# Twenty conditioning products moved out of the channel mixer into the stops around it, with the norms' root taken once per token

## What is computed

```
def rmsnorm(x, g):
    y = xf * lax.rsqrt(jnp.mean(xf * xf, axis=-1, keepdims=True) + RMS_EPS)
    return (y * g.astype(jnp.float32)).astype(x.dtype)
...
    for l in range(DEPTH):
        mod_x = (jax.nn.silu(c) @ w_ada[l] + b_ada[l])[:, None, :]
        mod_c = jax.nn.silu(c_ctx) @ w_ada[l] + b_ada[l]
        sh1, sc1, gt1, sh2, sc2, gt2 = jnp.split(mod_x, 6, axis=-1)
...
        hx = modulate(rmsnorm(x, g_pre_mix[l]), sh1, sc1)
        y_x, y_c = mixer_sublayer(hx, hc, ...)
        x = x + gt1 * rmsnorm(y_x, g_post_mix[l])
        hx = modulate(rmsnorm(x, g_pre_ffn[l]), sh2, sc2)
        x = x + gt2 * rmsnorm(channel_mixer(hx, l, ...), g_post_ffn[l])
```

## Time and profile before

| | us |
|---|---|
| median of 3 runs | 2317.41 (2314.95 to 2319.59) |
| the profiled execution | 2325.32 |
| its span, first to last instruction | 2323.5 |
| first mixer, up to the first stop | 0 to 578.6 |
| stop before the channel mixer | 578.6 to 605.0 |
| channel mixer | 605.0 to 1003.3 |
| stop behind it | 1003.3 to 1031.3 |
| second mixer | 1031.3 to 1356.3 |
| norms 5 and 6, router, gather | 1356.3 to 1391.2 |
| experts and end | 1391.2 to 2323.5 |

### The profile page before, as it was taken

The page is one execution under the profiler, slowest core; times in us unless marked ns, Lnnn a source line. Parts: engine busy times, 40 slices in busy tenths (PEclk is TensorE's granted clock), DMA queues, the critical chain, the costliest instruction groups (busy, mean ns, idle before and its releaser), DMA issues.

```text
span 2323.5 us, 55627 instructions
## 1 busy us (share of the span) xinstructions
PE 2260.5 (97%) x24638; PEld 1645.4 (71%) x24638; DVE 763.8 (33%) x1543; ACT 560.5 (24%) x1090; POOL 48.1 (2%) x63
## 2 busy tenths in 40 slices
PE   7999999999999999998999999999999999999999
PEld 4777877778678887868898986555555555555555
DVE  4465354543732223376647651000000000100002
ACT  4345343323322222234535430000000000000001
POOL 0000010000200000000011000000000000000000
PEclk8999999999999999999999989999999999999999
DMA  6323242224644344213333479999999999999992
GB/s 252 123 109 131 79 155 100 113 107 188 219 188 161 112 155 178 75 55 109 109 119 130 170 289 374 391 404 381 404 384 407 380 408 387 405 385 406 394 412 100
DMA packets 86185, 548.93 MB, mean 236 GB/s; under 512 B 10257, under 2 KB 13457, under 8 KB 25937
## 3 DMA queue, kind: packets, MB, share of 16 engines
q1 hardware_dynamic: 52880, 352.68, 39.4%
q10 hardware_dynamic: 28912, 178.14, 19.6%
q0 software_dynamic: 4176, 14.81, 2.0%
HBM read 529.08 MB, written 16.52 MB: 235 GB/s over the span
## 4 chain that ended last, share of the span: by engine, by line
PE 85%; DVE 9%; ACT 3%; issue 2%; DMA 1%; ACTq 0%; DVEq 0%; SPq 0%
PE S L1764 17%; PE O L1764 13%; PE pp L1439 9%; PE pp L1441 8%; PE pp L1440 8%; PE T L1764 8%; PE S L1439 2%; DVE wsp L971 2%; PE S L1440 2%; PE S L1441 2%; PE T L1440 2%; PE T L1441 2%; PE T L1439 2%; PE pp L1474 2%; PE T L1570 1%
## 5 line engine op out<-in xcount | busy, mean ns | idle before, releaser
L1764 PE MATMUL S<-slabs,M 128*32 128x256 f32 x7168 | 475.6, 380 | 1.4 <-issue 1.0
L971 DVE TENSOR_TENSOR wsp<-raw,wsp 128x1024 fp32r<-128x1024 f32 (+3 forms) x248 | 264.0, 1086 | 326.2 <-ACT wsp L631 325.0
L1764 PEld LDWEIGHTS S<-slabs,M 128*32 128x32 f32 x7168 | 231.3, 110 | 155.7 <-issue 13.4
L1439 PE MATMUL pp<-hx,wsp 128*128 128x512 f32 (+1 forms) x800 | 284.8, 356 | 20.2 <-DVE M L1182 4.7
L1764 PE MATMUL O<-slabs,M 128*32 128x256 f32 x5376 | 294.7, 379 | 0.0
L1394 DVE TENSOR_TENSOR M<-M,S 128x256 f32<-128x256 f32 x56 | 23.6, 421 | 807.0 <-ACT M L921 807.0
L1764 PE MATMUL T<-slabs,M 128*32 128x256 f32 x3584 | 279.2, 379 | 0.1
L1440 PE MATMUL pp<-hx,wsp 128*128 128x512 f32 (+1 forms) x800 | 277.4, 347 | 0.0
L1441 PE MATMUL pp<-hx,wsp 128*128 128x512 f32 (+1 forms) x800 | 277.3, 347 | 0.0
L1764 PEld LDWEIGHTS O<-slabs,M 128*32 128x32 f32 x5376 | 173.2, 110 | 114.9 <-issue 1.3
L631 ACT ACTIVATE wsp<-raw 128x1024 fp32r<-128x1024 f32 (+3 forms) x248 | 224.1, 935 | 30.7 <-PE pp L1441 19.6
(11 more groups left out here) (242 smaller groups left out, 2343.1 us busy)
## 6 DMA issues: line engine op xcount, KB each, us to landing
slabs<-in_w_moe SPq DMA_DIRECT2D x175, 1024.0 KB, 9.2
slabs<-in_w_moe ACTq DMA_DIRECT2D x161, 1024.0 KB, 9.2
raw<-in_w_main SPq DMA_DIRECT2D x84, 1024.0 KB, 5.0
M<-in_w_main SPq DMA_DIRECT2D x40, 1024.0 KB, 5.0
raw<-in_w_br SPq DMA_DIRECT2D x24, 512.0 KB, 3.6
xm<-in_w_main SPq DMA_DIRECT2D x8, 1024.0 KB, 5.2
raw<-in_w_dn SPq DMA_DIRECT2D x8, 768.0 KB, 4.2
moe_rows<-M POOLq DMA_DIRECT2D x14, 384.0 KB, 9.7
```

The costliest lines, as they stand in the source:

```text
L971: dve.tensor_tensor(wsp[:, slot, 1, 0:w], raw[:, rslot, half * w:half * w + w], wsp[:, slot, 0, 0:w], ALU.subtract).then_inc(lo_done, 1)
L1439: mm(dst, w_hi, x_hi, start=first, stop=False)
L1764: ins = mm(banks[g // 2][32 * c:32 * c + 32, 256 * (g % 2):256 * (g % 2) + 256], x(k, g), slab_e[i % RAW_E][:, 1024 * k + 256 * c:1024 * k ...
```

## The change

1. The 22 products and turns leave the channel mixer (`ffn`). Two of these slabs go beside the last tiles of the first mixer, whose plan now has 20 `ada` steps; the last turn stands before the output projection (`wout`).
2. Ten products and turns are written into each of the two stops (`stop`, `stop_product`, `stop_turn`), in place of most `keep_up` matmuls. Their slabs are loaded by `load_stop` into ten buffers of their own (`stop_buf`), some of which only come free when the stage before has ended.
3. In norms 1 to 6 the sum is taken with the squares as weights and one column of `mean` as data (`token_sums`), which leaves one number per token, 128 tokens down the partitions. Root and reciprocal then work on 4 columns (2 in norms 5 and 6). DVE multiplies the identity by each column (`dg`), and PE multiplies that by `mean` to spread the factors over all partitions into the PSUM bank `R` (`norm_cast`).
4. In norms 5 and 6 and in the router fewer constant matmuls stand in one block and more of them between the sums and the router's small matmuls.
5. POOL clears its scratch rows later (in the channel mixer), and three small DVE operations that prepare the second layer's factors stand behind norm 4.

```diff
+ADA_STOP = 10
+ADA_MIXER = [(0, s) for s in range(ADA_FIRST, ADA_SLABS)] + [(1, s) for s in range(ADA_SLABS - 2 * ADA_STOP)]
+STOP_PRODUCT = {0: 3, 1: 4, 2: 5, 4: 6, 5: 7}
+STOP_TURN = {0: 2, 1: 3, 2: 4, 3: 5, 5: 6, 6: 7}
...
             for g in range(2, N_SLABS):
+                if g == g_gu[0]:
+                    for n in range(4):
+                        load_stop(0, n, step_of[0, "wout", 0]["t"])
+                if g == g_gu[0] + 2:
+                    for n in range(4, ADA_STOP):
+                        load_stop(0, n, t_stop[0] if n < 8 else t_stop[0] + n - 7)
...
+                if g == g_mix[1] + 2:
+                    for n in range(6, ADA_STOP):
+                        load_stop(1, n, t_stop[1])
                 load(g)
...
+            def token_roots(n, N):
+                dve.wait_ge(sd_done, n + 1)
+                own.link(dve.reciprocal(root[:, 1, 0:N // P], root[:, 0, 0:N // P]))
+                for b in range(N // P):
+                    dve.tensor_scalar(dg[:, b, :], ident[:], root[:, 1, b:b + 1], float(D), ALU.mult, ALU.mult).then_inc(dg_done, 1)
+                dve.wait_ge(cast_done, n)
...
+            def token_sums(src, N, first, last):
+                for b in range(N // P):
+                    ins = mm(O[1][:, b:b + 1], src[:, P * b:P * b + P], mean[:, 0:1], ...)
...
+                token_sums(sq[:, 1, :], N, False, True).then_inc(sum_done, 4)
+                if n < 5:
+                    stop_product(n // 2, 0)
+                else:
+                    keep_up(5)
+                norm_cast(n, N)
...
+            def stop(b, n):
+                stop_product(b, 1)
+                stop_turn(b, 0)
+                stop_product(b, 2)
+                stop_turn(b, 1)
+                for k in range(KT):
+                    norm_sum(n, k, TOK)
+                    if k in STOP_PRODUCT:
+                        stop_product(b, STOP_PRODUCT[k])
+                    if k in STOP_TURN:
+                        stop_turn(b, STOP_TURN[k])
+                    if k in (3, 6):
+                        keep_up(2)
+                stop_product(b, 8)
+                norm_cast(n, TOK)
+                stop_product(b, 9)
+                stop_turn(b, 8)
+                keep_up(2)
+                stop_turn(b, 9)
...
             mixer(0, 1, 0)
-            keep_up(28)
-            for k in range(KT):
-                norm_sum(2, k, TOK)
-            keep_up(31)
+            stop(0, 2)
             ffn()
...
-            keep_up(16)
+            keep_up(6)
             for k in range(KT):
                 norm_sum(6, k, SEQ)
-            keep_up(31)
+                keep_up(5 if k == KT - 1 else 1)
+            norm_cast(6, SEQ)
+            keep_up(5)
...
-            ins.then_inc(rt_pe, 1)
+                if k == KT - 1:
+                    ins.then_inc(rt_pe, 1)
+                else:
+                    keep_up(1)
```

More of the change, by code:

```diff
@@ L128, in mixer_plan @@
             end = len(steps)
+    steps.extend(late)
     for n in range(0, KT, 2):
@@ L207, in build_program @@
         ada_c = view(M, 0, 2048)
-        ada_f = [view(M, 2048 * j, 2048) for j in range(2)]
+        ada_m = [view(M, 2048 * j, 2048) for j in range(2)]
+        stop_buf = [ada_m + [slabs[:, n, :] for n in (4, 5, 0, 1, 2, 3)] + ada_m,
+                    ada_m + [slabs[:, n, :] for n in (6, 7, 8, 9, 0, 1, 2, 3)]]
         def ada_rows(n):
@@ L331, in build_program @@
         g_gu, g_dn = [0, 0], [0, 0]
+        stop_main = [nmain, 0]
+        nmain += ADA_STOP
         for h in range(2):
             g_gu[h], u_gu[h] = len(order), units()
-            for _ in range(F_HALF[h]):
-                add("main", 1, 2048)
-                add("main", 1, 2048, True)
+            add("main", F_HALF[h], 2048)
             g_dn[h], u_dn[h] = len(order), units()
@@ L384, in build_program, with plan_stop @@
         t = ADA_FIRST
+        def plan_stop(b):
+            nonlocal t
+            t_stop[b], use_stop[b] = t, use[0]
+            t += ADA_STOP
+            for n in range(2):
+                use[n] += ADA_STOP // 2
         plan_mixer(0)
+        plan_stop(0)
         for h in range(2):
-            t_gu[h], use_gu[h] = t, use[0]
+            t_gu[h] = t
             for f in range(F_HALF[h]):
@@ L398, in build_program @@
                 use[b] += DN_STAGE // 2
+        plan_stop(1)
         plan_mixer(1)
@@ L416, in build_program @@
                 place(g, ada_c, 0, ada_use[ada_mix[n - 1]] if n > ADA_BESIDE_A else step_of[0, "vn", (1, 1)]["t"])
[L417 to L420, removed]
+        need = [max([last_use[n - 4] if n >= 4 else 0] + [ada_src[g][3] for g in ada_src if g < slab_of[n]]
+                    + ([step_of[0, "wout", 0]["t"]] if slab_of[n] >= g_gu[0] else [])) for n in range(N_UNITS)]
         end_of = [u_gu[0] + 2, N_UNITS]
@@ L710, in affine_step, with stop_row @@
                                    ).then_inc(affine, 1)
+            def stop_row(b, n):
+                act.wait_ge(tile_done, t_stop[b] + n + 1)
+                if n >= 2:
+                    act.wait_ge(cols_done, ADA_FIRST + ADA_STOP * b + n - 1)
+                act.activation(adr_f[:, n % 2, :], pp[n % 2][:, 0:256], ACT.Copy).then_inc(taken[n % 2], 1)
             def prenorm(n, l, which, N, hcount):
+                stop = {2: 0, 4: 1, 6: None}[n]
+                if stop is not None:
+                    stop_row(stop, 0)
+                    stop_row(stop, 1)
                 for k in range(KT):
@@ L1074, in prenorm @@
             def prenorm(n, l, which, N):
-                dve.wait_ge(sd_done, n + 1)
-                own.link(dve.reciprocal(rs[:, 0:N], sd[:, 0:N]))
+                token_roots(n, N)
                 for k in range(KT + 1):
@@ L1281, in _ @@
             postnorm(3, 0, 1, TOK, y)
-            dve.wait_ge(cols_done, ADA_FIRST + ADA_FFN)
-            own.link(mod_add(1, ADA_SLABS - ADA_FFN, O[0][:, 0:4 * ADA_FFN]))
-            for part in range(4):
+            dve.wait_ge(cols_done, ADA_FIRST + ADA_STOP)
+            own.link(mod_add(1, ADA_SLABS - 2 * ADA_STOP, O[0][:, 0:4 * ADA_STOP]))
+            for part in range(2):
                 own.link(am_part(1, part))
@@ L1457, in keep_up, with norm_cast @@
                     mm(bank[:, 0:P], mean[:], mean[:], start=True, stop=True)
+            def token_sums(src, N, first, last):
+                for b in range(N // P):
+                    ins = mm(O[1][:, b:b + 1], src[:, P * b:P * b + P], mean[:, 0:1], start=(first and b == 0), stop=(last and b == N // P - 1))
+                return ins
+            def norm_cast(n, N):
+                before = [0, 4, 8, 12, 16, 18][n - 1]
+                for b in range(N // P):
+                    pe.wait_ge(dg_done, before + b + 1)
+                    ins = mm(R[:, P * b:P * b + P], mean[:], dg[:, b, :], start=True, stop=True)
+                ins.then_inc(cast_done, 1)
@@ L1900, in _pack_dense @@
     dns, f = [], 0
+    for s in range(ADA_STOP):
+        ada(1, ADA_SLABS - 2 * ADA_STOP + s)
     for nF in F_HALF:
```

99 lines of the change are left out of this document (61 added, 38 removed).

## The result

The changed kernel takes 2323.65 us in the median of seven runs (2321.39 to 2327.73). The kernel before took 2317.3 us in seven runs on the same chip. The ratio is 1.0029 with a 95% interval of 1.0018 to 1.0039. I had forecast 2288.6 and a gain of 28.8 us. The change costs 6 us instead.

A forecast was written before the change was run, and what follows sets the result against it. PE was taken to bound most stages, the norms' ACT and DVE chain the old stops. -30.8 (channel mixer) + 6.0 (first mixer) + 4.2 (stops) - 8.2 (norms 5 and 6, router) = -28.8, from 2317.4 to 2288.6 us; range 2274 to 2303.

The forecast's parts named there:

- I take PE's sum, since each price is a row at full clock: Two stops: PE, not DVE, sets the pace, +2.1 us each, +4.2 for both.
- the last of the signs of being wrong: Stops: the prediction would be wrong if the clock there is below 1.00; it expected 1.00.
- my second rival: Stops: 12 us of each at clock 0.50 would cost 6, giving 2301 us; chance 0.12.
- The stops at full clock: Each stop +2.1 us: PE's pace costs +4.1, less 2.0 for the second root.
- the 2.3 among my signs: Stops: sums spaced at 2.3 us for the first blocks, as a sign in the profile after.
- The full drain on each side of a product: Stops: a pair of tiling-mode switches at 0.33 us, not 0.17; each stop 1.3 longer, result 2291.
- The root's gain: Stops: factors ready 2.1 us earlier at norm 1, 2.0 at norm 2; 4.1 a stop if nothing else changed.
- The channel mixer: Products and turns leave the tile boundaries: 28.8, 1.2 and 0.8 us, together -30.8.
- hidden work that turns into a wait: Channel mixer, behind a half's last tile: of 2.57 us only about 0.4 goes, since DVE's splitting chain ends late.
- The first mixer: Two more slabs in its last groups: +2.6, +1.3 and 2.1 us, sum +6.0; bounds 3.2 to 7.8.
- Norms 5 and 6 and the router: Roots 1.4 us, router pairs 4.5 earlier, gather 2.7, small steps about 1; sum -8.2.
- The loads: Stops: slabs land 5.0 us apart, no wait expected; rival of late loads, slower from 8.0 us spacing, chance 0.03.

The follow-up runs named there:

- norms_thin: Kernel before with slabs left in the channel mixer, norms merged with one-column sums, constants in the stops, router as changed; 2321.63 us, before 2317.73, ratio 1.0015.
- old_sums: Changed kernel with slabs still in the stops, but norms 1 to 4 as before (512-column sums, old roots); 2319.07 us, before 2321.18, ratio 0.9989.
- norms_wide: Same as norms_thin but with 128-column sums in the merged norms; 2307.92 us, before 2321.18, ratio 0.9943.
- wide_sums: Changed kernel with each sum of norms 1 to 6 multiplying by 128 equal columns, not one; 2300.27 us, before 2321.18, ratio 0.9913.
- twelve_bridged: twelve plus nine constants ahead of PE's wait behind each half of the channel mixer; 2295.21 us, before 2321.03, ratio 0.9883.
- more_constants: Changed kernel, thin sums kept, with two constants behind each of a stop's eight sums (16, not 4); 2313.31 us, before 2317.73, ratio 0.9976.
- twelve: wide_sums with twelve slabs in the second stop and none of the second layer's in the first mixer; 2293.73 us, before 2321.03, ratio 0.9882.
- wide_late_turn: wide_sums with the first mixer's last turn behind the first tile of the output projection; 2295.43 us, before 2317.73, ratio 0.9907.

## Why the prediction was wrong, point by point

**The step that failed** is "I take PE's sum, since each price is a row at full clock". The prices were nearly right and the clock was not. A clock below 1.00 in the stops was the last of the signs of being wrong that I had named. It is my second rival, "the clock falls in the stops", to which I gave 0.12, and it was mis-sized too. I had 12 us of each stop at 0.50, costing 6. The windows show 13.5 and 15.3 us lost. The slip in my 6 is plain: 12 us of work at half the clock take 24 and cost 12. PE sets the pace, so whatever it does at 0.50 takes twice as long. In the first stop that is some 13.5 us of work, from 597.4 to 624.7. The clock was back only behind the last thin sum of the stop, which ends at 621.27. So it was in the second stop (last sum's end 1034.7, full clock from 1037.2) and in both of norms_thin. With no thin sum ahead a fall was shorter: 6.6 us for the first of the second stop, 6 and 10 us behind the first gaps of old_sums. What brings the clock back was not tested. With 13.5 + 15.3 = 28.8 us lost in the stops in place of 12, that rival gives 2288.6 + 28.8 = 2317 and not 2301.

**Why I gave it 0.12.** I read 1.00 in the old stops and put it down to the constants. The old sums multiplied 512 columns each, and I priced their replacement by its time alone. That time hardly changes (0.96 us thin, 1.07 with 128 columns, about 1.1 for an old one), because weight loads fill a thin sum: they stretch over 0.97 us in norms_thin, where the sum's row is 0.95. What changes is how much is multiplied in it. norms_thin and norms_wide show this alone, with all products left out. The row that should have warned me is the earlier trace rows: there the same kind of row, eight columns wide, stood at 0.50. The Trainium skill, TensorE: Matmul & The Clock Gate, What's actually happening, says that the clock is set by how busy PE has been. The gap in old_sums agrees with that (3.01 us idle, then 0.52). But PE's busy time in the changed kernel's stops is 3.00 of 3.00 us at either level, so the busy column of a profile doesn't tell when this rule bites.

**The stops at full clock** were sized well. wide_sums has +2.6 and +2.7 where I had +2.1, and the changed kernel's less the clock's loss would have about +1.1 in each. Sum to sum my prices make 1.01 + 0.42 + 0.86 + 0.15 = 2.44 (the 2.3 among my signs left out the switches), and the rows have 2.43. The sum in them is dearer than I had it, 0.96 for 0.86, so that little is left for the switches. The full drain on each side of a product, which I weighed as 0.33 a pair, would make at least 2.62 and isn't there. The end of the stop came as described. These rows of wide_sums show the last sum, its root, and the scaling 2.1 us behind the sum's end (2.2 predicted), where before it was 4.15:

```profile
610.14 1.06 PE L1529 MATMUL O<-mean,M 128*128 128x128 f32 x8
611.23 0.26 ACT L703 ACTIVATE root<-O,eps 128x4 f32<-128x4 f32 x1 [2.39 <-PE O L1529]
...
613.32 0.87 DVE L1100 SCALAR_TENSOR_TENSOR M<-xm,am,S 128x256 f32<-128x256 f32 x2 [0.70 <-PE S L1537]
```

The root's gain is confirmed by norms_wide: stops of 22.7 us, 3.7 and 3.6 shorter, where I had 4.1.

**The channel mixer** was right: -29.2 for -30.8. The tiles are 10.88 us as predicted (10.9), which the timeline of the changed kernel shows, to be read beside the earlier trace rows:

```profile
653.43 0.39 PE L1506 MATMUL S<-hx,wsp 128*128 128x512 f32 x1
658.87 0.39 PE L1506 MATMUL T<-hx,wsp 128*128 128x512 f32 x1
664.31 0.39 PE L1506 MATMUL S<-hx,wsp 128*128 128x512 f32 x1
...
764.63 0.76 PE L1506 MATMUL pp<-opr,wsp 128*128 128x512 f32 x1 [2.25 <-DVE opr L1313]
```

The last row is the wait behind the first half. I had it as hidden work that turns into a wait, which is right. I had no price for what an idle PE does to the clock: the row takes 0.76 where its neighbours take 0.39, and the clock is 0.96 over the 40 us around it, 1.6 us. twelve_bridged gives this back. The wait behind the second half had no such fall here.

**The first mixer** cost +8.7 for +6.0. The full group takes 520.49 - 500.26 = 20.23 us (20.20 by the earlier trace rows). The tail is what I under-priced:

```profile
500.26 0.50 PE L1506 MATMUL pp<-hx,wsp 128*128 128x512 f32 x1 [1.46 <-DVE M L1280]
...
520.49 0.50 PE L1506 MATMUL pp<-hx,wsp 128*128 128x512 f32 x1 [1.45 <-DVE M L1280]
...
541.27 0.61 PE L1601 MATMUL pp<-sel,M 128*128 128x2 f32 x4 [1.99 <-DVE M L1280]
```

From 520.49 to the output projection at 541.74 it is 21.25 us, where I had 16.32 + 1.3 + 2.1 = 19.7. The turn waits for a DVE that is in the middle of splitting weights, and behind that wait the clock is 0.79 over 540 to 548, another 1.7.

**Norms 5 and 6 and the router** gave -3.5 to -4.9 (by which profile of before) for -8.2. With wide sums they gave -6.3 to -7.7, and -7.7 is against the profile that the prediction worked on. (My end of the router's pairs was 0.3 too early: 1369.3 and eight times 0.66 make 1374.6.) The missing part is again the clock, which falls among norm 6's thin sums, as the changed kernel's timeline shows:

```profile
1371.35 0.56 PE L1529 MATMUL O<-mean,M 128*128 128x1 f32 x4
1371.78 0.47 PE L1524 MATMUL T<-mean 128*128 128x128 f32 x2
1372.08 0.78 PE L1529 MATMUL O<-mean,M 128*128 128x1 f32 x4
1372.72 0.77 PE L1524 MATMUL T<-mean 128*128 128x128 f32 x2
```

Behind it the gather ran at full clock, in 3.7 us (3.4 predicted).

**The loads** were never late: no sum or product of either stop waited for one in any version. In the first stop seven slabs were issued together, six of its own and one for `raw`, and came at 420 GB/s, 2.5 us each, half of the 5.0 that I took from the earlier trace rows. That row is a latency, not a spacing.

**The whole account**: predicted -28.8, measured +6.4, 35.2 apart. In the stretches that is 12.5 + 14.2 (stops), 4.7 (router), 2.7 (first mixer), 1.6 (channel mixer), -0.5. Read as clock, the losses in the changed kernel are 13.5 + 15.3 in the stops, 30.06 x 0.11 = 3.3 at the router, 8 x 0.21 = 1.7 in the first mixer and 40 x 0.04 = 1.6 in the channel mixer, 35.4 together. That the two sums come so close is in part luck. They are not made of quite the same parts (in the first mixer 1.0 of the 2.7 is a longer wait, and the stops without the clock's loss would have been about 1 us each below my price), and by the first profile of before the measured side would be smaller by 3.7. But nearly all that I got wrong is clock.

What stays open: what would hold the clock in every execution at the least cost, and what decides when it comes back. more_constants shows an edge at which the same program goes either way, and norms_wide, twelve and twelve_bridged still lose the clock near the router in the profiles taken.

## What to carry to other kernels

When narrow matmuls replace wide ones, check the clock and not only the time, even where the wide ones compute something: they may be what holds it. If the time is set by weight loads, make the narrow ones wide again with columns that nobody reads; here that turned a loss of 0.3% into a gain of 0.9%, and a better place for two slabs made it 1.2%. Price a fall of the clock in a stretch that PE paces by work, not by time: what PE does at half the clock costs its own length once more. In these runs that went on behind the last of the narrow sums (13.5 us in the first stop), and behind the first gaps of old_sums, with wide sums, it was 3 to 5 us.

## What the runs showed of the hardware

- A sum of four matmuls with weights of their own takes 0.96 us with one column and 1.07 with 128. With the second the granted clock was 1.00 in both stops of all six profiles taken. With the first it fell in seven of the eight stops profiled (both of the changed kernel twice, both of norms_thin, one of more_constants).
- The clock goes either way near an edge: more_constants, one program, took 2304.5 to 2305.3 us in four executions and 2313.1 to 2313.6 in five.
- The clock also falls at a gap: with sums of 512 columns, PE idle for 3.0 or 3.4 us, it fell at all four such gaps of old_sums; at a wait of 1.98 to 1.99 us in the first mixer it fell in the changed kernel and wide_sums and not in wide_late_turn.
- The same experts took 927.9 to 928.0 us in five profiles and 931.9 to 933.0 in eight.
